# Experts' rows in pairs on ScalarE and TensorE, and adaLN's products summed on VectorE, in a two-layer hybrid encoder trunk

## The reference

```
cond = silu(c)
for l in range(2):
    mod = cond @ w_ada[l] + b_ada[l]                    # (6 * 1024): shifts, scales and gates
    h = rms(x) * (1 + sc_m) + sh_m
    ... = split(h @ w_in[l])                            # 6868 columns
    y_a = gla(...); y_b = dsa(...); y_c = rwkv7(...)    # three chunk-causal mixers, 512 wide each
    x = x + gt_m * ((g_a * (y_a @ w_a) + g_b * (y_b @ w_b) + g_c * (y_c @ w_c)) @ w_out[l])
    x = x + gt_f * peer(rms(x) * (1 + sc_f) + sh_f)
return rms(x) * g_final

def peer(h):    # 512 tokens, 8 heads, 16 experts of 16384 for each head
    s1, s2 = top-16 of each half's 128 sub-keys; e_idx, gate = top-16 of the 256 sums, softmax
    act = gelu(einsum('thkd,td->thk', u[e_idx], h))     # one dot product of 1024 for each expert
    return einsum('thk,thkd->td', gate * act, v[e_idx])
```

## Time and profile before

| | us |
|---|---|
| median of 3 runs | 4078.35 (4077.44 to 4078.89) |
| profiled execution, its own time | 4096.53 |
| its span | 4094.5 |

### The profile page before, as it was taken

One profiled execution on the slowest core, in us unless ns is written; L12 is line 12 of the kernel. 1 busy time (PEld: TensorE's weight loads), 2 busy tenths in 40 slices (PEclk: granted clock), 3 DMA queues, 4 the chain that ended last, 5 costly groups with the idle time before them and its releaser, 6 DMA issues.

```text
span 4094.5 us, 63355 instructions
## 1 busy us (share of the span) xinstructions
PE 3004.4 (73%) x22136; PEld 1869.3 (46%) x22136; DVE 2476.3 (60%) x6188; ACT 1631.2 (40%) x4715; POOL 1167.0 (29%) x1076
## 2 busy tenths in 40 slices
PE   7989987657889895758788887557988894444444
PEld 4676874324545573425546565225555561001001
DVE  1432319986457728986555538986468549955444
ACT  2214113553454523553464424533553533333333
POOL 2100002343333301343333311333323312443332
PEclk8879998768789996867889998678989996555555
DMA  9702346999999955999999976889999976999997
GB/s 355 265 2 98 119 134 253 395 367 356 347 370 407 359 208 214 381 366 346 362 376 391 371 285 230 334 344 355 387 363 385 383 298 270 398 402 421 421 420 316
DMA packets 235294, 1315.56 MB, mean 321 GB/s; under 512 B 21216, under 2 KB 35168, under 8 KB 103904
## 3 DMA queue, kind: packets, MB, share of 16 engines
q0 software_dynamic: 160512, 1124.14, 69.3%
q1 hardware_dynamic: 74464, 187.38, 12.7%
HBM read 1309.34 MB, written 2.10 MB: 320 GB/s over the span
## 4 chain that ended last, share of the span: by engine, by line
PE 39%; DVE 21%; DMA 21%; ACT 7%; issue 7%; DVEq 2%; ACTq 1%; POOL 1%; another core or an unknown queue 0%; POOLq 0%; SPq 0%
DMA row<-uv,e_idx 19%; DVE row L1546 8%; PE bank L693 8%; PE bank L707 7%; PE bank L625 6%; PE bank L960 4%; PE bank L1026 3%; DVE reg L1443 2%; PE bank L797 1%; DVE reg L1438 1%; PE bank L879 1%; ACT e_diag L1121 1%; ACT e_wg L1119 1%; PE bank L637 1%; DVE reg L1448 1%
## 5 line engine op out<-in xcount | busy, mean ns | idle before, releaser
L1965 POOL DMA_INDIRECT row<-uv,e_idx x1024 | 1130.8, 1104 | 2755.2 <-PE bank L625 1872.0
L1546 DVE CUSTOM_DVE_ANT_0 row<-row,e_rep 128x1024 f32<-128x1024 f32 x1024 | 1239.8, 1225 | 760.6 <-DMA row<-uv,e_idx 699.3
L625 PE MATMUL bank<-row,e_diag 128*32 128x256 f32 x8192 | 836.1, 505 | 805.9 <-ACT e_diag L1121 769.2
L625 PEld LDWEIGHTS bank<-row,e_diag 128*32 128x32 f32 x8192 | 204.3, 125 | 1349.6 <-ACT e_diag L1121 1058.1
L1117 ACT ACTIVATE e_ge<-e_dot 128x1 f32<-128x1 f32 x1024 | 205.6, 201 | 1271.1 <-DVE e_dot L1546 1186.5
L707 PE MATMUL bank<-hT,weights 128*128 128x256 f32 (+2 forms) x2176 | 530.3, 401 | 33.1 <-ACT hT L1189 23.6
L707 PEld LDWEIGHTS bank<-hT,weights 128*128 128x128 f32 (+2 forms) x2176 | 414.7, 195 | 150.8 <-issue 43.4
L693 PE MATMUL bank<-hT,weights 128*128 128x256 f32 x1536 | 359.8, 386 | 2.2 <-ACTq L1379 2.0
L1121 ACT ACTIVATE e_diag<-mask,e_wg 128x32 f32<-128x32 f32 x1024 | 329.2, 321 | 74.0 <-issue 3.8
L1119 ACT ACTIVATE e_wg<-e_gate,e_ge 128x1 f32<-128x1 f32 x1024 | 301.5, 294 | 73.8 <-issue 3.5
L693 PEld LDWEIGHTS bank<-hT,weights 128*128 128x128 f32 x1536 | 289.7, 192 | 64.0 <-issue 23.4
(11 more groups left out here) (273 smaller groups left out, 3587.7 us busy)
## 6 DMA issues: line engine op xcount, KB each, us to landing
row<-w_ada POOLq DMA_DIRECT2D x48, 1024.0 KB, 9.8
weights<-w_mac SPq DMA_DIRECT2D x64, 768.0 KB
weights<-w_in SPq DMA_DIRECT2D x44, 1024.0 KB
weights<-w_mb SPq DMA_DIRECT2D x32, 768.0 KB
weights<-w_out SPq DMA_DIRECT2D x16, 1024.0 KB
weights<-w_pq SPq DMA_DIRECT2D x16, 1024.0 KB
row<-uv,e_idx POOLq DMA_INDIRECT x1024
weights<-w_in SPq DMA_DIRECT2D x8, 1056.0 KB
```

The lines of the kernel that those rows point to most:

```text
L625: last = mm(acc_ps[g % 2][c * QT:(c + 1) * QT, 0:2 * P], e_diag[:, n % RING, :], row[n % RING][:, D + c * 2 * P:D + (c + 1) * 2 * P], star ...
L1546: V.tensor_tensor_reduce(row[r][:, 0:D], row[r][:, 0:D], e_rep[g % 2], 1.0, 0.0, ALU.mult, ALU.add, e_dot[:, r:r + 1]).then_inc(dots, 1)
L1965: pool.indirect_dma_start(row[r], None, uv, bass.IndirectOffsetOnAxis(ap=e_idx[:, j:j + 1], axis=0)).then_inc(rows_landed[r], 16)
```

## The change

- ScalarE waits for the dots of two rows, then does one gelu over both columns, two scalings by the gate and two diagonals, and signals once (`diag_ready` counts pairs). Even rows have no step of their own any more.
- TensorE waits for a pair and does the eight matmuls of both rows in one step; it still signals `rows_summed` after each row. GpSimd is unchanged.
- The last 20 adaLN groups are no longer multiplied on TensorE. `ada_sum` on VectorE multiplies each of a group's eight 128x512 slices with its column of cond and adds them up in `a_sum` (one tensor_scalar, seven scalar_tensor_tensor, a drain after each), in four steps of two operations. It frees the two buffers, waits for the columns of the group two before (its `a_sum` is used again), and signals `ad_summed`. TensorE keeps `ada_columns`, with a column of ones; ScalarE has no adaLN step in lap 0.
- All step tables are new. TensorE has 20 steps in lap 0 (before 40) and 151 in each later lap (before 278 or 279), ScalarE none and 155 (before 20 and 283), VectorE 82 and 288 (before 2 and 288).

```diff
 STEPS = {
     "PE": (
-        "00000000000201100000023100302100000010010000001200022101010000105001000001000110000100000001",
...
+        "00000000000000011000011010010100000000000100000001000000000000019001",
...
     "ACT": (
-        "00000001000100104000000000110000100001010100100000000000203001",
...
+        "",
...
     "DVE": (
-        "00000000000000000010000000000000000000000000000000000000000000000000000000000000000000000000000001",
...
+        "00020263130632000004030101000000112000013000002752400068200000001",
...
@@ TensorE, expert_steps
-                    pe.wait_ge(diag_ready, n + 1)
-                    for c in range(4):
-                        last = mm(acc_ps[g % 2][c * QT:(c + 1) * QT, 0:2 * P], e_diag[:, n % RING, :],
-                                  row[n % RING][:, D + c * 2 * P:D + (c + 1) * 2 * P], start=(s == 0), stop=(s == USLOTS - 1))
-                    last.then_inc(rows_summed, 1)
+                    if s % 2 == 0:
+                        continue
+                    pe.wait_ge(diag_ready, (n + 1) // 2)
+                    for m, s_ in ((n - 1, s - 1), (n, s)):
+                        for c in range(4):
+                            last = mm(acc_ps[g % 2][c * QT:(c + 1) * QT, 0:2 * P], e_diag[:, m % RING, :],
+                                      row[m % RING][:, D + c * 2 * P:D + (c + 1) * 2 * P], start=(s_ == 0), stop=(s_ == USLOTS - 1))
+                        last.then_inc(rows_summed, 1)
                     yield True
@@ TensorE, ada_steps
-                for n in range(ADA_FIRST, L * ADA + 1):
-                    pe.wait_ge(ad_copied, n)
-                    if n < L * ADA:
-                        ada_strips(acc_ps[0], n, ad_filled)
-                        yield True
-                    if n > ADA_FIRST:
-                        if n - 1 == ADA:
-                            pe.wait_ge(mod_taken, 1)
-                        ada_columns(acc_ps[1][:, 4 * n - 4:4 * n], n - 1).then_inc(mod_filled, 1)
-                        yield True
+                for n in range(ADA_FIRST, L * ADA):
+                    if n == ADA:
+                        pe.wait_ge(mod_taken, 1)
+                    pe.wait_ge(ad_summed, n - ADA_FIRST + 1)
+                    ada_columns(acc_ps[1][:, 4 * n:4 * n + 4], n, ones[:, 0:1]).then_inc(mod_filled, 1)
+                    yield True
@@ ScalarE, expert_steps
+                    if s % 2 == 0:
+                        continue
                     act.wait_ge(dots, n + 1)
-                    A(e_ge[:, r:r + 1], e_dot[:, r:r + 1], ACT.Gelu)
+                    A(e_ge[:, r - 1:r + 1], e_dot[:, r - 1:r + 1], ACT.Gelu)
                     act.drain()
+                    A(e_wg[:, r - 1:r], e_gate[:, j - 1:j], ACT.Copy, scale=e_ge[:, r - 1:r])
                     A(e_wg[:, r:r + 1], e_gate[:, j:j + 1], ACT.Copy, scale=e_ge[:, r:r + 1])
                     act.drain()
+                    A(e_diag[:, r - 1, :], mask, ACT.Copy, scale=e_wg[:, r - 1:r])
                     A(e_diag[:, r, :], mask, ACT.Copy, scale=e_wg[:, r:r + 1]).then_inc(diag_ready, 1)
                     yield True
@@ ScalarE, ada_steps
-                for n in range(ADA_FIRST, L * ADA):
-                    act.wait_ge(ad_filled, n - ADA_FIRST + 1)
-                    A(a_sum[n % 2], acc_ps[0][:, :], ACT.Copy)
-                    act.drain().then_inc(ad_copied, 1)
-                    yield True
@@ VectorE
+            def ada_sum(n, kh, k0):
+                b, to = 2 * n + kh, a_sum[n % 2]
+                w = v3(row[b % RING], 4)
+                if kh == 0 and k0 == 0:
+                    if n < ADA_FIRST + 2:
+                        last = (0, "mod", n - 2)
+                        dve.wait_ge(B.filled(last), B.turn(last) + 1)
+                    else:
+                        dve.wait_ge(mod_filled, n - 1 - ADA_FIRST)
+                if k0 == 0:
+                    dve.wait_ge(ada_landed[b % RING], 16 * (b // RING + 1))
+                for k in (k0, k0 + 1):
+                    if kh == 0 and k == 0:
+                        V.tensor_scalar(to, w[:, 0, :], cond[:, 0:1], None, ALU.mult)
+                    else:
+                        last = V.scalar_tensor_tensor(out=to, in0=w[:, k, :], scalar=cond[:, 4 * kh + k:4 * kh + k + 1], in1=to, op0=ALU.mult, op1=ALU.add)
+                        if k == 3:
+                            last.then_inc(ada_used[b % RING], 1)
+                    if kh and k == 3:
+                        dve.drain().then_inc(ad_summed, 1)
+                    else:
+                        dve.drain()
+
             def ada_steps():
                 for l in range(L):
                     first = 0 if l else ADA_FIRST
+                    for g in range(first, ADA):
+                        for kh in range(2):
+                            for k0 in (0, 2):
+                                ada_sum(ADA * l + g, kh, k0)
+                                yield True
```

More of the change, by code:

```diff
@@ new lines @@
+        "200000000072100000005000000001101043000000403000000109400120110201100100102000220010200210002100001001011001020030000"
+        "100000007100001004000000010211011010202000001000010020010001010001210000020000101111000100001000101000000100010002000"
+        "010200010001600000000000000101000000022002",
+        "002000b00011110000010000000000600000010000000310000043800410211101100100101010121001110110011110002000011001010003000"
+        "010000008100010004000001001401001100021010000010000001000002001001001001001110001200120100010300000011000101000100002"
@@ L288 @@
+        "0010001001011000021110112000002",
     ),
     "DVE": (
[L290 to L293 removed]
@@ new lines @@
+        "100g50001c0403010103481000302700004400b000000100001130011010101010010100100201010011001101110111000011101010001102100"
+        "211010001011010100020010002001101010102301002006101010480004310031002036201110400020010000000001001001000142000004000"
+        "1000101000001002010000000100101102002a00040000220002170003002309",
+        "10p143022000100034000410000081001210004301042247000010000100510101100101001101010101011000210201000011101010001011101"
+        "101210010001101010001002110010101100030300005640000026003141102201103900110000010000010020030000001100000100200020001"
@@ L638, in ada_strips, with ada_columns @@
                     last.then_inc(done if kh else ada_used[b % RING], 1)
-            def ada_columns(ps, n):
+            def ada_columns(ps, n, rows):
                 for j in range(4):
-                    last = mm(ps[:, j:j + 1], a_sum[n % 2][:, j * P:(j + 1) * P], sc[:, 4:5], start=True, stop=True)
-                    if j == 0:
+                    last = mm(ps[:, j:j + 1], a_sum[n % 2][:, j * P:(j + 1) * P], rows, start=True, stop=True)
+                    if n < ADA_FIRST and j == 0:
                         last.then_inc(ada_used[(2 * n + 1) % RING], 1)
@@ L1139, in _ @@
                 modc = modc_all[:, 48 * l:48 * l + 48]
-                turns = Turns(expert_steps(lap - 1) if lap else ada_steps(), STEPS["ACT"][lap])
+                turns = Turns(expert_steps(lap - 1), STEPS["ACT"][lap]) if lap else Turns()
                 def cl(name, i=0, n=1):
```

57 lines of the change are left out of this document (24 added, 33 removed).

## The result

The changed kernel took 4100.43 us (median of 5, 4095.19 to 4112.22), 1.0056 times the kernel before, with a 95% interval of 1.0035 to 1.0077: slower by 0.56%, 23 us on 4078. I had forecast 30 us less. Run once more, with the fourth group of experiments, the changed kernel had a ratio of 1.0061 [1.0041, 1.0081].

A forecast was written before the change was run, and what follows sets the result against it. Laps were taken as bound by the loop of six row buffers, only the tail by transfers; -60 (laps) + 28 (first lap) + 2 (tail) = -30 us on 4078 gave 4048 us, range 4010 to 4085.

The forecast's parts named there:

- Part 5: First lap: VectorE's adaLN sums put the first mask 38 us later, about 10 given back, net +28 us.
- Part 4: Laps 1 to 3: with the new step tables a lap takes 896 us against 916, -60 us for three.
- Part 3: Row buffers: a pair's hold costs 0.08 us a row, 21 us a lap; in the tail nothing but 2 us.
- Parts 1 to 3: Laps: ScalarE's pairs save 5 us a lap, TensorE's 15, the longer buffer hold costs 21; they nearly cancel.
- Part 2: TensorE in the laps: joining two rows' matmuls saves 20 us busy, 15 us a lap on the path.
- Rival (a): Middle of laps 1 to 3: the pair's buffer hold shows in full, 0.17 to 0.35 us a row; 4154 us, chance 0.17.
- (b): Laps don't move, savings and hold cancel, tables worth nothing; the first lap's 28 us stay: 4108 us, chance 0.25.
- (c): First lap: the summing on VectorE runs hidden under the transfers as TensorE gets ahead: 4020 us, chance 0.12.
- (d): Laps: ScalarE's and TensorE's relief counts in full, less the ring's 21 us: -47 us a lap, 3967 us, chance 0.12.
- the marks laid down: Mask about 210 us, first fetch 680, new operation 0.75, laps near 896, TensorE's row 0.65, tail interval 2.5, under 65 table loads.
- the two signs of being wrong: Laps' row interval outside 3.2 to 3.35 us, or the recurrence's first mask before 180 us.

The follow-up runs named there:

- fourth group of experiments: Four kernels on one chip: both engines in pairs with single tail (0.9922), ScalarE alone in pairs with single tail (0.9917), changed kernel (1.0061), changed kernel with TensorE single (1.0038).
- adaLN alone: The kernel before with adaLN's 20 groups summed on VectorE and the new tables of lap 0, single rows and old tables behind: 4119.28 us, 1.0090.
- the spread version: Changed kernel with single rows and only adaLN groups 4 to 12 ahead of the recurrence on VectorE, the rest under the trunk's matmuls: 4023.84 us, 0.9864.
- the parts together: Changed kernel with ScalarE paired only in laps 1 to 3, TensorE single, only adaLN groups 4 to 12 ahead of the recurrence: 4005.48 us, 0.9868.

## Why the prediction was wrong, step by step

**The step that failed first is Part 5, the first lap**: what it gave back behind the mask. It does not fail alone. Of the 53 us between the forecast of -30 and the measured +23, 19 are here, 18 at the tables (Part 4) and 16 at the pairs, 13 of these in the tail (Part 3).

Four profiles with VectorE's sums ahead of the mask (the changed kernel twice, with TensorE single, and adaLN alone) stand against nine with adaLN as before and six buffers. First mask: 213 against 171, +42, forecast +38. First fetch: 675 to 683 against 632 to 644, means 679.7 and 637.5, +42. The forecast subtracted 10 us that the lap should give back behind the mask. By these means the stretch from mask to fetch is 466 us with VectorE's sums and 466 without: nothing comes back. In the 28 us behind the mask TensorE is busy 21.6 us in place of 26.4, and yet the way to the fetch is no shorter; why, no run isolates. Further on TensorE is busy 387 of 434 us, so that the start is carried through. 28 us were 42, and by the ratios 37 to 47. The step's arithmetic of VectorE (6.3 us a group, 126 in all) was right. What I did not ask is whether the work has to stand there. With its groups spread the first fetch comes 18 us earlier than with the strips (616.5 against 634.2 on one chip).

**Part 3, the tail.** "In the tail it costs nothing" was wrong: 2 us forecast, 13 to 15 measured. Seven profiles with six buffers and a pair on either engine in the tail have 702 to 710 us, nine with single rows 689 to 694 (means 706 and 691). The reserve was counted with 2.5 us for a transfer: 10.3 of 14.9 us. Measured with four buffers, the pair's loop is 13.6, so that 1.3 us are left of the 14.9 (the single row's loop of 11.6 leaves 3.3). The loss shows where VectorE also does the routing pieces, in the first 200 us of the tail; that their delays use up the reserve fits this place, but no run isolates it. Here is the experts' matmul of the changed kernel, of ScalarE alone in pairs, and of single rows:

```profile
3392.00:3592.00 200.00, 59.32 (x508) 18.91 (x512) 0.53 0.91 352
```

```profile
3318.00:3518.00 200.00, 61.71 (x512) 19.20 (x512) 0.54 0.90 353
```

```profile
3337.00:3537.00 200.00, 70.97 (x544) 14.01 (x544) 0.54 0.93 373
```

63.5 and 64 rows against 68: 4.5 rows of 2.94 us are 13 us. Later the transfers are full again (share 1.00 at 411 GB/s, 2.51 us a row) and nothing more is lost. The Trainium skill (DMA: Bandwidth & Descriptors, Anatomy of one DMA) has a fixed 2.0 us and the bytes over 436 GB/s, an estimate of 4.4 us for a row alone, which was nearer than my 2.5. The four-buffer tail has 7.3 us as a mean (5.8 and 6.9 in the chain) with two others under way, and the measurement decides.

**Parts 1 to 3 in the laps.** Savings and hold were forecast to cancel, and about do. Four profiles with both pairs (three kernels) have laps of 2720.7, 2717.4, 2695.5 and 2707.7, mean 2710; two with single rows 2693.7 and 2718.4 (the spread version), mean 2706; five with ScalarE alone in pairs 2679 to 2690. But the signs are not those of the working: ScalarE's pair, counted 5 us a lap, gives 3 (by the ratios, less the tail's 13) to 7 (by the means of the profiles), though its table loads are 70 with and without it (they come from the tables, not from the pairing). TensorE's pair, counted as a gain of 15 us a lap, is a loss of 1 to 8. That term of Part 2 failed in its mechanism: the busy time of a row falls from 0.70 to 0.67 us with ScalarE's pair alone, and joining the steps on TensorE takes off nothing more. What is left of it is the wait: in the laps the changed kernel waits 452 us for diagonals in its second profile, with TensorE single 440. At such a place the pair's first row starts one diagonal later, and is no longer summed while ScalarE makes the second; that this is the whole loss is argued from the order of the steps, not measured. Rival (a), the hold in full, is refuted at six buffers. With four the pairs do cost 113 us over 768 rows, 0.15 us a row: the hold is there and shows once the ring is short.

**Part 4, the tables.** Forecast 60 us; measured 42 by the ratios, 55 by the profile of single rows at the new places (3.28 us a row against 3.34, ends of 59 us against 63). The mechanism stands, a little smaller. Not foreseen: the tables and the pairs belong together. The pairs at the old tables cost 132 us (1.0324). By the profile of the changed kernel the laps gave 32 us in place of 60: their ends came as forecast, and the row's interval was 3.31 us as a mean in place of 3.26.

**Sum.** Forecast -60 + 28 + 2 = -30; by the ratios -42 + 47 + 18 = +23. Each term came out worse. The rivals: (b) named this sign and 4108, but for another reason, since the laps did move: that its number is near is luck. (c), the summing hidden, falls with the mask at 213, and (d), 47 us less a lap, with laps that are 11 us shorter. Of the marks laid down, the mask, the first fetch (674.9 of 680), the operation of 0.75 us, TensorE's row and the interval held; the tail's interval held only in its second part, the laps near 896 (mean 906) and the table loads did not. Neither of the two signs of being wrong appeared (interval outside 3.2 to 3.35, mask before 180), though the forecast was wrong: they watched only two of the terms. I took the fetch at 675 to 680 for a loss of 28 us, because I compared it with the 652 of one profile.

## What to carry to other kernels

Before work is moved to an idle engine, ask what stands ahead of it at that point of its fixed order: the same 160 operations on VectorE cost 42 us when all stood ahead of the recurrence, and gained 18 us when half of them lay under the matmuls behind it. If rows are batched at all, then on the engine whose result is waited for anyway (ScalarE, in the laps, for 3 to 7 us a lap), not on the one that frees the buffer. Where a ring's reserve decides, take the transfer's time from a run with fewer buffers, not from the interval of a full queue. Best of the runs are the spread version (0.9864) and the parts together (0.9868), 1.3 to 1.4% under the kernel before. Their intervals don't tell them apart, and the first has no pairs at all: the gain is in where the steps stand, the sums on VectorE included.

## What the hardware showed beyond that

A gather of 1 MB has an interval of 2.5 us in a full queue, and takes 7.3 us as a mean from issue to landing (5.8 and 6.9 in the chain shown) when only two others are under way. And where work was moved away from TensorE, the granted clock was lower: ahead of the mask 0.90 with the strips (busy 117 of 128 us), 0.79 in the spread version (77 of 105) and 0.67 in the changed kernel (99 of 170); the laps had 0.84 to 0.86, before 0.83 to 0.86.
